# Hybrid attention layer on one core: two VectorE operations moved in the linear-attention steps, and the first projection begun on two token tiles

## The chip, the cores and the metric

The kernel runs on one core of a Trainium2 chip. The metric is device time in microseconds, from the start to the end of one execution; the median of several executions is given. TensorE multiplies matrices out of SBUF into PSUM, VectorE (DVE), ScalarE (ACT) and GpSimd (POOL) work elementwise, and SyncE (SP) issues the transfers. Each engine takes its instructions in order, and engines wait for one another through semaphores.

## The reference

One encoder layer on 1024 tokens of width 1024, all in float32. What matters here is the first part:

```python
h = rmsnorm(x, norm_mix_w[l])
proj = h @ w_in[l]
gq, gk, gv, ggate, ga, dq, dk, dv, dgate = split_cols(proj)
g = jax.nn.log_sigmoid((ga @ w_alpha2[l] + b_alpha2[l]).astype(f32)) / GLA_TAU
o_gla = gla_chunked(gq, gk, gv, g)          # chunks of 64 tokens, 4 heads
o_gla = head_rmsnorm(o_gla, gla_norm_w[l]) * jax.nn.silu(ggate)
# inside gla_chunked, per chunk
scores = jnp.where(causal, q_dec @ k_inv.T, 0.0)
o = scores @ v + q_dec @ state
state = decay * state + (k * jnp.exp(G_last - G)).T @ v
```

Behind it come differential attention over 4 heads, an output projection with residual, cross-attention into 256 memory tokens with its projections, and a last RMSNorm.

## The kernel before

Tokens are worked in 8 tiles of 128 (TT), the model width in 8 parts of 128 (KT). Each float32 operand of a large product is split in a high part and a low part: ScalarE writes the high part, VectorE subtracts it from the source for the low part (`lo_part`), and TensorE makes three matmuls (`mm3`): high by high, high by low, low by high. A weight matrix comes in tiles of 128x512, loaded by SP into a ring of four (`w_raw`) and split into a ring of 13 (`w_hi`, `w_lo`); a slot of `w_raw` is loaded again when the low part of the tile four before is done.

The order of the whole program is one list of stages, `PLAN`, written by `stages()` with the weight tiles (`("w", n)`) put in by `with_weights()`. Every engine walks through this one list and issues its own share of each stage, so the place of a stage in the list sets its place in each engine's queue. The stages that matter here:

- `("sq", t)`, `("scale", t)`: squares of input tile t (ScalarE), variance (VectorE), its root (GpSimd), scaling (VectorE). `("tr", t, half)`: four transposes on TensorE, high part on ScalarE, low part on VectorE, into `actT_hi` and `actT_lo`.
- `("busy", part, n)`: n transposes of the identity on TensorE, which nobody reads.
- `("pos",)`, `("vec",)`: positions converted on VectorE; norm weights, gate bias and positions turned on TensorE and copied to `vecs` and `pos_f` on VectorE. Every weight tile is scaled by a column of `vecs`.
- `("const",)`: the 16 gate columns of `w_in`, scaled and split into `ga_both`. `("ga", n)`: product of `ga_both` with 512 tokens. `("z", n)`: gate logits, `("gate", n)`, `("gsum", n)`, `("gexp", n)`: log-sigmoid, running sums and exponentials.
- `("G0", n, k)`: part k of the projection of q and k of the linear attention, for 512 tokens, into four PSUM banks.
- Linear attention in 16 steps (`GLA_STEPS`): two pairs of heads, eight tiles of 128 tokens each. Per step s: `("sc", s)`, scores on TensorE, their masked copy out of PSUM on VectorE (`sc_f`), high part on ScalarE, low part on VectorE; `("kv", s)`, chunk states; `("qk", s + 1)` and `("kdT", s + 1)`, operands of the next step; `("proj", s + 1)`, projection of the next values and gate path (24 matmuls of 512 columns) into `bank0`, of which ScalarE takes v's high part and the tanh and VectorE v's low part; `("gmul", s + 1)`, the gate, after which `bank0` is free for the next projection; `("o", s)`, the output product, its sum out of PSUM (`o_f`) and squares; `("ovar", s)`, variance (`var_o`), with the root on GpSimd; `("ofin", s)`, output scaled by root and gate (`mix_out`, two operations), which SP stores to memory.

TensorE issues `kv` of a step only when v's low part is there (`v_dve`), and a projection when the gate before is done (`pj_dve`).

Of the kernel before, what the change touches and what calls it, by code (L numbers as in the profile page):

```python
# [23 lines left out]
F32 = mybir.dt.float32  # L24
# [54 lines left out]
def stages():  # L79
# [4 lines left out]
    def normed(t):  # L84
        return [("sq", t), ("scale", t)]

    def busy(part, n):
        return [("busy", part, n)]

    plan = [("zeros",), *normed(0), ("sq", 1), ("scale", 1), *normed(2), *busy(0, 24), *tr(0), *busy(1, 2), ("sq", 3), *tr(1)]  # L90
    plan += [("pos",), ("scale", 3), *busy(2, 4), *tr(2), *busy(3, 6), ("vec",), ("const",), *tr(3), *busy(4, 20), ("w", 0), ("w", 1), *normed(4), ("w", 2), *normed(5), ("ga", 0)]
    plan += [("w", 3), *normed(6), ("w", 4), *normed(7), ("G0", 0, 0), ("z", 0), ("gate", 0), ("G0", 0, 1), *tr(4)]
# [278 lines left out]
def build(nc, a, out):  # L371

    with ExitStack() as ctx:
# [78 lines left out]
        ga_both = sb("ga_both", [P, KT, P], F32R, zone_a)  # L452
# [72 lines left out]
        sq_sum, var_ok, rs_ok, scaled = sem("in_squares"), sem("in_var"), sem("in_rsqrt"), sem("in_scaled")  # L525
        tr_pe, tr_act, tr_dve = sem("inT_pe"), sem("inT_hi"), sem("inT_lo")
# [112 lines left out]
        def _(sp):  # L639
# [13 lines left out]
            for t in range(4):  # L653
                load_input(t)
# [10 lines left out]
            for n in range(2):  # L665
                load_weight(n)
# [67 lines left out]
        def _(pool):  # L734
# [15 lines left out]
            for stage in PLAN:  # L750
                kind, *w = stage
                if kind == "sq":
# [20 lines left out]
        def _(act):  # L773
# [21 lines left out]
            for stage in PLAN:  # L795
                kind, *w = stage
                if kind == "sin":
                    act.wait_ge(dve_c, 3)
# [11 lines left out]
                elif kind == "w":  # L810
# [5 lines left out]
                    if n == 7 * KT + 2 * 2 * KT:  # L816
                        act.wait_ge(dve_c, 5)
# [173 lines left out]
        def _(dve):  # L991
# [14 lines left out]
            for stage in PLAN:  # L1006
                kind, *w = stage
                if kind == "zeros":
                    dve.memset(ga_both[:, :, 2 * RANK:P].bitcast(F32), 0.0)
# [14 lines left out]
                elif kind == "const":  # L1024
                    dve.wait_ge(d_ga, 16 * 3)
                    then_wait(dve.tensor_tensor(ga_raw[:, :, :], ga_raw[:, :, :],
                                                nw_mix[:, :].unsqueeze(2).to_broadcast([P, KT, RANK]), ALU.mult))
                    ga_hi, ga_lo = ga_both[:, :, 0:RANK], ga_both[:, :, RANK:2 * RANK]
                    then_wait(dve.tensor_copy(ga_hi, ga_raw[:, :, :]))
                    lo_part(ga_lo, ga_raw[:, :, :], ga_hi).then_inc(dve_c, 1)  # L1030
# [132 lines left out]
                elif kind == "sc":  # L1163
# [5 lines left out]
                    last.then_inc(sc_cp, 1)  # L1169
                    dve.wait_ge(sc_act, s + 1)  # L1170
# [39 lines left out]
                elif kind == "proj":  # L1210
# [3 lines left out]
                    if i == 0:  # L1214
                        dve.wait_ge(dve_c, 4)
# [131 lines left out]
        def _(pe):  # L1347
# [56 lines left out]
            for stage in PLAN:  # L1404
# [21 lines left out]
                elif kind == "ga":  # L1426
                    n = w[0]
                    pe.wait_ge(dve_c, 1)
# [3 lines left out]
                    for k in range(KT):  # L1432
                        pe.matmul(banks[3], ga_both[:, k, :], actT_hi[:, k, c], start=k == 0, stop=False)
                        last = pe.matmul(banks[3], ga_both[:, k, :], actT_lo[:, k, c], start=False, stop=k == KT - 1)
                    last.then_inc(ga_pe, 1)
                elif kind == "z":
# [4 lines left out]
                    last.then_inc(z_pe, 1)  # L1441
                elif kind == "G0":
                    n, k = w
                    t = slice(512 * n, 512 * n + 512)
# [5 lines left out]
                    for c in range(4):  # L1450
                        if k == 0:
                            wait(pe, g0_dve, 4 * n + c - 3)
                        last = mm3(banks[4 + c], w_hi[:, k, cols(c)], w_lo[:, k, cols(c)],
                                   actT_hi[:, k, t], actT_lo[:, k, t], k == 0, k == KT - 1)
# [255 lines left out]
```

## Time and profile before

| what | value |
|---|---|
| median of 3 runs | 870.24 us (870.15 to 870.57) |
| profiled execution, own time | 874.1 us |
| its span | 872.4 us |
| TensorE busy | 850.4 us (97%) |
| VectorE busy | 529.6 us (61%) |
| ScalarE busy | 397.2 us (46%) |
| GpSimd busy | 44.1 us (5%) |
| granted TensorE clock, mean | 0.996 of 2.4 GHz |

The median stems from runs without a profile, all durations and starts from the one profiled execution, whose time is 3.9 us above the median. A timeline gives for each instruction its start from the begin of the span, its duration, engine and source line, and in brackets how long the engine sat idle ahead of it and for whom. PEld is the loading of TensorE's stationary operand. Many instructions overlap the one before on the same engine, so the distance of two starts can be shorter than a duration.

### The profile page before, as it was taken

The page shows a single profiled execution, that of the slowest core. Times are in us where ns is not written, and L with a number is a line of the kernel's source. Part 1 is how long each engine was busy: PE and PEld are TensorE (multiplying, and loading weights), DVE is VectorE, ACT ScalarE, POOL GpSimd, SP SyncE. Part 2 cuts the span into 40 slices and gives each one's busy share as a digit, 9 for nine tenths or more (in the row PEclk, how much of TensorE's full clock was granted, in tenths as well). Part 3 has the DMA queues.
Part 4 walks back from the last instruction along what each step waited for, and adds up shares of the span by engine and source line. Part 5 has one row for each costly group of instructions (what it writes and reads, how often), then busy time and mean ns, then how long its engine had stood idle before and what let it go on. Part 6 is the DMA issues. An engine that isn't in the chain of part 4 may idle for free.

```text
span 872.4 us, 12997 instructions
## 1 busy us (share of the span) xinstructions
PE 850.4 (97%) x4676; PEld 705.0 (81%) x4676; DVE 529.6 (61%) x1274; ACT 397.2 (46%) x982; POOL 44.1 (5%) x84
## 2 busy tenths in 40 slices
PE   7999999999999999999999899999999999999997
PEld 6777877777788888888878887888888888888885
DVE  6667667767578668678768765223336654355543
ACT  7765444444346345445545655203425543234422
POOL 2000000000000000000000000000100000010001
PEclk9999999999999999999999999999999999999999
DMA  8321112112212112102112266521022202351112
GB/s 270 110 78 37 31 41 69 37 43 67 59 31 55 35 34 56 34 22 67 43 63 74 88 213 216 184 86 61 32 89 74 68 29 73 97 192 49 49 49 97
DMA packets 53592, 67.69 MB, mean 78 GB/s; under 512 B 5844, under 2 KB 32536, under 8 KB 53528
## 3 DMA queue, kind: packets, MB, share of 16 engines
q1 hardware_dynamic: 53528, 66.85, 24.2%
q8 instruction: 38, 0.62, 0.3%
q14 instruction: 26, 0.21, 0.1%
HBM read 58.44 MB, written 8.39 MB: 77 GB/s over the span
## 4 chain that ended last, share of the span: by engine, by line
PE 78%; DVE 11%; ACT 4%; issue 3%; DMA 3%; POOL 0%; SPq 0%; POOLq 0%; ACTq 0%
PE bank L1350 12%; PE bank L1352 12%; PE bank L1351 12%; PE banks2to L1350 8%; PE banks2to L1352 8%; PE banks2to L1351 8%; PE banks6to L1401 4%; PE banks2to L1573 4%; PE bank L1599 2%; DVE w_lo L1004 2%; DVE state L1183 1%; ACT junk L789 1%; ACT w_hi L793 1%; DMA tile_a<-mixed 1%; DVE mix_out L1207 1%
## 5 line engine op out<-in xcount | busy, mean ns | idle before, releaser
L1350 PE MATMUL bank<-w_hi,actT_hi 128*128 128x512 f32 x472 | 189.8, 402 | 1.2 <-DVE gate L1161 0.3
L1352 PE MATMUL bank<-w_hi,actT_lo 128*128 128x512 f32 x472 | 184.5, 391 | 0.0
L1351 PE MATMUL bank<-w_lo,actT_hi 128*128 128x512 f32 x472 | 184.3, 390 | 0.0
L1004 DVE SCALAR_TENSOR_TENSOR w_lo<-w_raw,vecs,w_hi 128x512 fp32r<-128x512 f32 x120 | 86.6, 747 | 43.5 <-ACT w_hi L793 43.5
L1350 PEld LDWEIGHTS bank<-w_hi,actT_hi 128*128 128x128 f32 x472 | 88.9, 188 | 22.2 <-DVE gate L1161 3.5
L1352 PEld LDWEIGHTS bank<-w_hi,actT_lo 128*128 128x128 f32 x472 | 88.6, 188 | 19.2
L1351 PEld LDWEIGHTS bank<-w_lo,actT_hi 128*128 128x128 f32 x472 | 88.9, 188 | 16.6
L793 ACT ACTIVATE w_hi<-w_raw,vecs 128x512 fp32r<-128x512 f32 x120 | 82.4, 717 | 11.8 <-DMA w_raw<-in_w_cq 6.1
L1350 PE MATMUL banks2to<-w_hi,actT_hi 128*128 128x512 f32 x168 | 66.5, 396 | 0.0
L1352 PE MATMUL banks2to<-w_hi,actT_lo 128*128 128x512 f32 x168 | 65.6, 390 | 0.0
L1351 PE MATMUL banks2to<-w_lo,actT_hi 128*128 128x512 f32 x168 | 65.5, 390 | 0.0
L933 ACT ACTIVATE prob<-banks2to,neg_maxs 128x128 f32<-128x128 f32 (+7 forms) x64 | 46.9, 740 | 14.2 <-DVE neg_maxs L1247 13.9
L748 POOL TENSOR_TENSOR rs_o<-var_o,neg_half 128x1 f32<-128x1 f32 (+1 forms) x48 | 28.6, 596 | 413.0 <-DVE var_o L1272 271.8
L789 ACT ACTIVATE junk<-x_res 128x1024 bf16<-128x1024 f32 (+1 forms) x17 | 17.1, 1007 | 65.1 <-DVE x_res L1296 65.0
L1246 DVE TENSOR_REDUCE neg_max<-banks2to 128x2 f32<-128x256 f32 (+7 forms) x32 | 43.3, 1352 | 3.9 <-PE banks2to L1573 3.3
L1296 DVE TENSOR_TENSOR x_res<-banks2to,x_res 128x512 f32<-128x512 f32 x17 | 11.7, 691 | 46.8 <-PE banks2to L1352 46.8
L1350 PE MATMUL banks2to<-actT_hi,w_hi 128*128 128x512 f32 x96 | 38.8, 404 | 0.0
L1352 PE MATMUL banks2to<-actT_hi,w_lo 128*128 128x512 f32 x96 | 37.5, 391 | 0.0
L1351 PE MATMUL banks2to<-actT_lo,w_hi 128*128 128x512 f32 x96 | 37.4, 390 | 0.0
L1352 PEld LDWEIGHTS banks2to<-w_hi,actT_lo 128*128 128x128 f32 x168 | 31.5, 188 | 6.7
L793 ACT ACTIVATE qk_tok<-bank 128x192 f32<-128x192 f32 x28 | 9.3, 331 | 60.7 <-PE bank L1352 60.6
L1296 DVE TENSOR_TENSOR x_res<-bank,x_res 128x512 f32<-128x512 f32 x15 | 10.4, 691 | 43.4 <-PE bank L1352 43.4
(288 smaller groups left out, 1818.9 us busy)
## 6 DMA issues: line engine op xcount, KB each, us to landing
w_raw<-in_w_in SPq DMA_DIRECT2D x56, 256.0 KB, 2.9
w_raw<-in_w_ckv SPq DMA_DIRECT2D x32, 256.0 KB, 3.4
w_raw<-in_w_cq SPq DMA_DIRECT2D x32, 256.0 KB, 2.8
w_raw<-in_w_co SPq DMA_DIRECT2D x32, 256.0 KB, 2.7
stage_in<-in_x SPq DMA_DIRECT2D x8, 512.0 KB, 4.9
tile_a<-mixed SPq DMA_DIRECT2D x16, 256.0 KB, 3.6
w_raw<-in_w_out SPq DMA_DIRECT2D x16, 256.0 KB, 3.1
x_res<-in_x SPq DMA_DIRECT2D x8, 512.0 KB, 4.9
```

The lines of the kernel that those rows point to most:

```text
L748: pool.tensor_tensor(dst, src, neg_half[:, 0:n], ALU.pow).then_inc(sem_out, 1)
L789: act.activation(junk[:, 0:n], src, ACT.Square, accum_out=total).then_inc(sem_done, 1)
L793: return act.activation(dst, src, ACT.Copy, scale=scale)
L933: last = act.activation(prob[:, m, 0:n], wide[:, 2 * m:2 * m + 2, :].rearrange("p j c -> p (j c)")[:, 0:n], ACT.Exp, scale=DQK ** -0.5, bi ...
L1004: return dve.scalar_tensor_tensor(dst, src, scale, hi.bitcast(F32), ALU.mult, ALU.subtract)
L1246: then_wait(dve.tensor_reduce(neg_max[:, i % 2, :], both, AX.X, ALU.max, negate=True))
L1296: dve.tensor_tensor(x_res[:, t, c], ps, x_res[:, t, c], ALU.add).then_inc(pr_dve, 1)
L1350: pe.matmul(dst, l_hi, r_hi, start=start, stop=False)
L1351: pe.matmul(dst, l_hi, r_lo, start=False, stop=False)
L1352: return pe.matmul(dst, l_lo, r_hi, start=False, stop=stop)
L1401: last = pe.transpose(ps[:, cols(j)], src, ident[:, :])
L1573: last = pe.matmul(wide[:, 2 * half + g // 512, 0:keys.stop - g], l[rows, 0, cols(t)], r[rows, 1, keys], start=m == 0, stop=m == 2)
```

## The change

Three edits. In the linear-attention steps the scores' masked copy is a stage of its own, `("scp", s)`, ahead of `("ovar", s - 1)`, and `("ofin", s - 1)` stands ahead of `("proj", s + 1)`. At the start the first two parts of the q and k projection are done on two token tiles (256 tokens) first, as `("G0h", k)`, ahead of the gate projection, and their `("G0", 0, k)` covers the other 256 tokens; the stages around are put in another order, the fourth input tile is loaded behind the small vectors and the first weight tile, and there are 42 instead of 56 filler transposes. The splitting of the gate weights goes from VectorE to GpSimd, and `ga_both` has 32 columns instead of 32 and 96 zeros.

```diff
-    plan = [("zeros",), *normed(0), ("sq", 1), ("scale", 1), *normed(2), *busy(0, 24), *tr(0), *busy(1, 2), ("sq", 3), *tr(1)]
-    plan += [("pos",), ("scale", 3), *busy(2, 4), *tr(2), *busy(3, 6), ("vec",), ("const",), *tr(3), *busy(4, 20), ("w", 0), ("w", 1), *normed(4), ("w", 2), *normed(5), ("ga", 0)]
-    plan += [("w", 3), *normed(6), ("w", 4), *normed(7), ("G0", 0, 0), ("z", 0), ("gate", 0), ("G0", 0, 1), *tr(4)]
+    plan = [("zeros",), *normed(0), *normed(1), ("sq", 2), *busy(0, 24), ("tr", 0, 0), ("pos",), ("scale", 2), ("tr", 0, 1)]
+    plan += [*busy(1, 2), ("tr", 1, 0), ("vec",), ("tr", 1, 1), *busy(2, 6), ("sq", 3), ("w", 0), ("tr", 2, 0), ("scale", 3)]
+    plan += [("tr", 2, 1), *busy(3, 10), ("G0h", 0), ("w", 1), *tr(3), ("G0h", 1), ("w", 2), ("const",)]
+    plan += [*normed(4), ("w", 3), *normed(5), ("ga", 0)]
+    plan += [("G0", 0, 0), ("z", 0), *normed(6), ("w", 4), *normed(7), ("gate", 0), ("G0", 0, 1), *tr(4)]
...
     for s in range(GLA_STEPS):
+        plan.append(("scp", s))
         if s:
             plan.append(("ovar", s - 1))
...
-            plan.extend([("proj", s + 1), *passed, ("gmul", s + 1), ("o", s)])
+            plan.extend([*passed, ("proj", s + 1), ("gmul", s + 1), ("o", s)])
...
-        ga_both = sb("ga_both", [P, KT, P], F32R, zone_a)
+        ga_both = sb("ga_both", [P, KT, 2 * RANK], F32R, zone_a)
...
+                if kind == "const":
+                    pool.wait_ge(d_ga, 16 * 3)
+                    pool.wait_ge(vec_dve, 1)
+                    pool.tensor_tensor(ga_raw[:, :, :], ga_raw[:, :, :],
+                                       nw_mix[:, :].unsqueeze(2).to_broadcast([P, KT, RANK]),
+                                       ALU.mult).then_inc(ga_pool, 1)
+                    pool.wait_ge(ga_pool, 1)
+                    pool.tensor_copy(ga_both[:, :, 0:RANK], ga_raw[:, :, :]).then_inc(ga_pool, 1)
+                    pool.wait_ge(ga_pool, 2)
+                    pool.tensor_tensor(ga_both[:, :, RANK:2 * RANK], ga_raw[:, :, :],
+                                       ga_both[:, :, 0:RANK].bitcast(F32), ALU.subtract).then_inc(ga_pool, 1)
...
+                elif kind == "G0h":
+                    k = w[0]
+                    if k == 0:
+                        pe.wait_ge(tr_dve, at("tr", 1, 1))
+                        pe.wait_ge(vec_dve, 1)
+                    pe.wait_ge(w_dve, k + 1)
+                    for c in range(4):
+                        mm3(banks[4 + c][:, 0:256], w_hi[:, k, cols(c)], w_lo[:, k, cols(c)],
+                            actT_hi[:, k, 0:256], actT_lo[:, k, 0:256], k == 0, False)
```

How instructions stand on the engines. TensorE at the start, before the change, from the third input tile (`stage_in`) to the gate projection (`ga_both`):

```order
L1423 MATMUL bank<-ident,stage_in 128x128 x8
L1409 MATMUL banks6to<-ident 128x128 x6
L1414 MATMUL banks2to<-ident,vec_rows 128x28
L1415 MATMUL banks2to<-ident,pos_rows 128x8
L1423 MATMUL banks2to<-ident,stage_in 128x128 x8
L1409 MATMUL banks6to<-ident 128x128 x20
L1433 MATMUL banks2to<-actT_hi,ga_both 128x512
L1434 MATMUL banks2to<-actT_lo,ga_both 128x512
```

And after it, from the first half of the second input tile to the first matmuls of a half projection (`w_hi`), 12 of them for each of the two:

```order
L1433 MATMUL banks2to<-ident,stage_in 128x128 x4
L1424 MATMUL banks2to<-ident,vec_rows 128x28
L1425 MATMUL banks2to<-ident,pos_rows 128x8
L1433 MATMUL banks2to<-ident,stage_in 128x128 x4
L1419 MATMUL banks6to<-ident 128x128 x6
L1433 MATMUL bank<-ident,stage_in 128x128 x8
L1419 MATMUL banks6to<-ident 128x128 x10
L1360 MATMUL banks2to<-actT_hi,w_hi 128x256
L1361 MATMUL banks2to<-actT_lo,w_hi 128x256
L1362 MATMUL banks2to<-actT_hi,w_lo 128x256
```

The vectors' transposes moved into the second input tile's, and the half projections stand where the gate projection stood, which now follows the second of them.

VectorE in a linear-attention step with one weight tile, before the change:

```order
L1004 SCALAR_TENSOR_TENSOR w_lo<-w_raw,vecs,w_hi 128x512
L1197 TENSOR_SCALAR var_o<-sq_o 128x2
L1167 COPY_PREDICATED sc_f<-gla_mask,banks2to 128x128 x2
L1003 TENSOR_TENSOR sc_lo<-sc_f,sc_hi 128x256
L1183 SCALAR_TENSOR_TENSOR state<-state,decay,banks2to 128x256 x2
L1003 TENSOR_TENSOR st<-state,st 128x256 x2
L1003 TENSOR_TENSOR q_lo<-q_dec,q_hi 128x2x64
L1003 TENSOR_TENSOR k_lo<-k_inv,k_hi 128x128
L1003 TENSOR_TENSOR ke_lo<-bank,ke_hi 128x128
L1003 TENSOR_TENSOR v<-bank,v 128x256
L1207 SCALAR_TENSOR_TENSOR mix_out<-o_f,rs_o,gate 128x128 x2
L1161 SCALAR_TENSOR_TENSOR gate<-tanh_g,bank 128x256
```

And after it:

```order
L1020 SCALAR_TENSOR_TENSOR w_lo<-w_raw,vecs,w_hi 128x512
L1175 COPY_PREDICATED sc_f<-gla_mask,banks2to 128x128 x2
L1207 TENSOR_SCALAR var_o<-sq_o 128x2
L1019 TENSOR_TENSOR sc_lo<-sc_f,sc_hi 128x256
L1193 SCALAR_TENSOR_TENSOR state<-state,decay,banks2to 128x256 x2
L1019 TENSOR_TENSOR st<-state,st 128x256 x2
L1019 TENSOR_TENSOR q_lo<-q_dec,q_hi 128x2x64
L1019 TENSOR_TENSOR k_lo<-k_inv,k_hi 128x128
L1019 TENSOR_TENSOR ke_lo<-bank,ke_hi 128x128
L1217 SCALAR_TENSOR_TENSOR mix_out<-o_f,rs_o,gate 128x128 x2
L1019 TENSOR_TENSOR v<-bank,v 128x256
L1169 SCALAR_TENSOR_TENSOR gate<-tanh_g,bank 128x256
```

Two pairs changed places: `sc_f` and `var_o`, and `mix_out` and v's low part.

## Rows read from the trace of the kernel before

**Rows 1.** Page, part 1: busy time (share of the span) and instructions of each engine.

```profile
PE 850.4 (97%) x4676; PEld 705.0 (81%) x4676; DVE 529.6 (61%) x1274; ACT 397.2 (46%) x982; POOL 44.1 (5%) x84
```

**Rows 2.** Timeline 0 to 30 us, TensorE: start, duration (us), engine, line, operation, out<-in.

```profile
17.76 0.47 PE L1433 MATMUL banks2to<-actT_hi,ga_both 128*128 128x512 f32 x1 [0.29 <-DVE actT_lo L1003]
...
26.21 0.50 PE L1350 MATMUL banks2to<-actT_hi,w_hi 128*128 128x512 f32 x1
...
29.07 1.03 PE L1423 MATMUL bank<-ident,stage_in 128*128 128x128 f32 x8
```

**Rows 3.** Timeline 0 to 30 us, the other engines; in brackets idle time before.

```profile
9.21 1.06 ACT L793 ACTIVATE actT_hi<-bank 128x512 fp32r<-128x512 f32 x2
...
10.16 1.05 ACT L789 ACTIVATE junk<-stage_in 128x1024 bf16<-128x1024 f32 x1
...
12.24 0.55 POOL L748 TENSOR_TENSOR rs_in<-var_in,neg_half 128x1 f32<-128x1 f32 x1 [2.12 <-DVE var_in L1074]
...
13.40 0.73 DVE L1079 TENSOR_SCALAR stage_in<-stage_in,rs_in 128x1024 f32<-128x1024 f32 x1
...
15.55 0.28 DVE L1026 TENSOR_TENSOR ga_raw<-ga_raw,vecs 128x128 f32<-128x128 f32 x1
15.86 1.33 ACT L793 ACTIVATE w_hi<-w_raw,vecs 128x512 fp32r<-128x512 f32 x2
...
16.33 1.28 DVE L1003 TENSOR_TENSOR actT_lo<-banks2to,actT_hi 128x512 fp32r<-128x512 f32 x2
...
17.53 1.41 DVE L1004 SCALAR_TENSOR_TENSOR w_lo<-w_raw,vecs,w_hi 128x512 fp32r<-128x512 f32 x2
```

**Rows 4.** Timeline 121.5 to 138 us: a linear-attention step with one weight tile, from gate to gate.

```profile
125.41 0.42 DVE L1161 SCALAR_TENSOR_TENSOR gate<-tanh_g,bank 128x256 f32<-128x256 f32 x1
...
128.62 0.16 DVE L1197 TENSOR_SCALAR var_o<-sq_o 128x2 f32<-128x2 f32 x1
128.69 0.49 DVE L1167 COPY_PREDICATED sc_f<-gla_mask,banks2to 128x128 f32<-128x128 uint32 x2
...
132.18 0.38 ACT L866 ACTIVATE tanh_g<-bank 128x256 f32<-128x256 f32 x1
...
132.30 0.28 DVE L1003 TENSOR_TENSOR ke_lo<-bank,ke_hi 128x128 fp32r<-128x128 f32 x1
...
132.59 0.42 DVE L1003 TENSOR_TENSOR v<-bank,v 128x256 fp32r<-128x256 f32 x1
...
132.93 0.60 DVE L1207 SCALAR_TENSOR_TENSOR mix_out<-o_f,rs_o,gate 128x128 f32<-128x128 f32 x2
...
133.12 0.51 PE L1509 MATMUL banks2to<-v,ke_hi 64*128 64x256 f32 x4
...
133.57 0.42 DVE L1161 SCALAR_TENSOR_TENSOR gate<-tanh_g,bank 128x256 f32<-128x256 f32 x1
...
134.05 0.19 PEld L1350 LDWEIGHTS bank<-w_hi,actT_hi 128*128 128x128 f32 x1 [0.24 <-DVE gate L1161]
```

**Rows 5.** VectorE's gates, by their source line: durations (min/median/max ns), first and last start.

```profile
L1161 DVE SCALAR_TENSOR_TENSOR gate<-tanh_g,bank x16: 410/420/422, 85.3 to 206.8; 128x256 f32<-128x256 f32 x16
```

**Rows 6.** Timeline 108 to 118.5 us: a step without a weight tile.

```profile
109.81 0.50 PE L1350 MATMUL bank<-w_hi,actT_hi 128*128 128x512 f32 x1
...
116.27 0.42 DVE L1003 TENSOR_TENSOR v<-bank,v 128x256 fp32r<-128x256 f32 x1 [1.05 <-ACT tanh_g L866]
...
117.36 0.33 PE L1466 MATMUL bank<-ident,k_end 128*128 128x128 f32 x1
...
117.73 0.50 PE L1350 MATMUL bank<-w_hi,actT_hi 128*128 128x512 f32 x1
```

**Rows 7.** Timeline 141 to 152 us: ScalarE in the step with three weight tiles.

```profile
146.25 0.42 ACT L793 ACTIVATE sc_hi<-sc_f 128x256 fp32r<-128x256 f32 x1 [0.64 <-DVE sc_f L1167]
```

**Rows 8.** Timeline 650.9 to 654 us, TensorE: first 256-column score matmul, and what follows 24 of them.

```profile
651.00 0.28 PE L1350 MATMUL banks2to<-ck_hi,cq_hi 128*128 128x256 f32 x1
...
653.87 0.40 PE L1350 MATMUL bank<-actT_hi,w_hi 128*128 128x512 f32 x1
```

More of the change, by code:

```diff
@@ L525, in build @@
         sq_sum, var_ok, rs_ok, scaled = sem("in_squares"), sem("in_var"), sem("in_rsqrt"), sem("in_scaled")
+        ga_pool = sem("gate_weights_split")
         tr_pe, tr_act, tr_dve = sem("inT_pe"), sem("inT_hi"), sem("inT_lo")
@@ L651, in load_weight @@
                     sp.dma_start(dst, src).then_inc(d_raw[n % NRAW], 16)
-            for t in range(4):
+            for t in range(3):
                 load_input(t)
@@ L664, in _ @@
                 sp.dma_start(dst, src).then_inc(d_vec, 16)
-            for n in range(2):
-                load_weight(n)
+            load_weight(0)
+            load_input(3)
+            load_weight(1)
             for dst, src in (
@@ L751, in _ @@
                 kind, *w = stage
-                if kind == "sq":
+                if kind == "const":
[9 more added lines that the diff above has]
+                                       ga_both[:, :, 0:RANK].bitcast(F32), ALU.subtract).then_inc(ga_pool, 1)
+                elif kind == "sq":
                     c = slice(w[0], w[0] + 1)
@@ L797, in _ @@
                 if kind == "sin":
-                    act.wait_ge(dve_c, 3)
+                    act.wait_ge(dve_c, 2)
                     act.activation(sin2[:, :, :, :], ang2[:, :, :, :], ACT.Sin).then_inc(act_c, 1)
@@ L816, in _ @@
                     if n == 7 * KT + 2 * 2 * KT:
-                        act.wait_ge(dve_c, 5)
+                        act.wait_ge(dve_c, 4)
                     _, scale = weight_tile(n)
@@ L1008, in _ @@
                 if kind == "zeros":
-                    dve.memset(ga_both[:, :, 2 * RANK:P].bitcast(F32), 0.0)
                     dve.memset(row_pick[:, :], 0.0)
@@ L1023, in _ @@
                     dve.tensor_copy(pos_f[:, :], banks[5][:, 28:36]).then_inc(vec_dve, 1)
[L1024 to L1030, printed above, removed]
                 elif kind == "ang":
@@ L1162, in _ @@
                                              bank0[:, 256:512], ALU.add, ALU.mult).then_inc(pj_dve, 1)
-                elif kind == "sc":
+                elif kind == "scp":
                     s = w[0]
@@ L1169, in _ @@
                     last.then_inc(sc_cp, 1)
+                elif kind == "sc":
+                    s = w[0]
                     dve.wait_ge(sc_act, s + 1)
@@ L1214, in _ @@
                     if i == 0:
-                        dve.wait_ge(dve_c, 4)
+                        dve.wait_ge(dve_c, 3)
                     dve.wait_ge(pj_act, s + 1)
@@ L1427, in _ @@
                     n = w[0]
-                    pe.wait_ge(dve_c, 1)
+                    pe.wait_ge(ga_pool, 3)
+                    pe.wait_ge(d_ga, 16 * 3)
                     pe.wait_ge(tr_dve, at("tr", 4 * n + 3, 1))
@@ L1432, in _ @@
                     for k in range(KT):
-                        pe.matmul(banks[3], ga_both[:, k, :], actT_hi[:, k, c], start=k == 0, stop=False)
-                        last = pe.matmul(banks[3], ga_both[:, k, :], actT_lo[:, k, c], start=False, stop=k == KT - 1)
+                        pe.matmul(banks[3][0:2 * RANK, :], ga_both[:, k, :], actT_hi[:, k, c],
+                                  start=k == 0, stop=False)
+                        last = pe.matmul(banks[3][0:2 * RANK, :], ga_both[:, k, :], actT_lo[:, k, c],
+                                         start=False, stop=k == KT - 1)
                     last.then_inc(ga_pe, 1)
@@ L1441, in _ @@
                     last.then_inc(z_pe, 1)
+                elif kind == "G0h":
[7 more added lines that the diff above has]
+                            actT_hi[:, k, 0:256], actT_lo[:, k, 0:256], k == 0, False)
                 elif kind == "G0":
                     n, k = w
-                    t = slice(512 * n, 512 * n + 512)
+                    half = ("G0h", k) in NTH and n == 0
+                    t = slice(512 * n + 256 * half, 512 * n + 512)
                     if k == 0:
@@ L1452, in _ @@
                             wait(pe, g0_dve, 4 * n + c - 3)
-                        last = mm3(banks[4 + c], w_hi[:, k, cols(c)], w_lo[:, k, cols(c)],
-                                   actT_hi[:, k, t], actT_lo[:, k, t], k == 0, k == KT - 1)
+                        last = mm3(banks[4 + c][:, 256 * half:512], w_hi[:, k, cols(c)], w_lo[:, k, cols(c)],
+                                   actT_hi[:, k, t], actT_lo[:, k, t], k == 0 and not half, k == KT - 1)
                         if k == KT - 1 and n + c < 4:
```

## The prediction

> **What bounds the kernel now.** I read the page first: TensorE is busy 850.4 us of a span of 872.4 us [rows 1], and with 97% there is no stage in which another engine sets the time for long. What can be won is what TensorE spends at the start without real work, and the small gaps between its stages. So I read next the timeline of the first 30 us [rows 2, 3], and then the timeline of the linear-attention steps [rows 4 to 7], because the change touches these two stretches alone.
>
> The start: the first matmul that computes something is that of the gate projection at 17.76 us [rows 2]. Until then TensorE turns input tiles and otherwise turns the identity to stay busy, and these filler turns count as busy. What it waits for is a chain on ScalarE and VectorE: squares, scaling, high parts, low parts. The last link before 17.76 is the low part of the fourth token tile, 16.33 to 17.6 us, and directly ahead of it VectorE prepares the gate weights from 15.55 us [rows 3].
>
> The linear-attention steps: VectorE's gates start between 85.3 and 206.8 us, sixteen of them [rows 5]. A step that also prepares one weight tile takes 133.57 - 125.41 = 8.16 us [rows 4]. By the program there are ten of these behind the second gate, three steps without a tile (117.73 - 109.81 = 7.92 us from projection to projection [rows 6]), and one with three tiles. Inside a step the chain is gate, sum of the output's halves, squares, w_hi, w_lo, variance, masked scores' copy, sc_hi, and so on until v's low part, mix_out, gate. In a step of 8.16 us TensorE starts the next projection at 134.05, 0.06 us behind the end of the gate (133.57 + 0.42) [rows 4], and the row says that it sat idle for 0.24 us until that gate. So this loop is set by VectorE and ScalarE, not by TensorE.
>
> **The change, part one: the start.** First the times up to the first half projection. ScalarE has the squares of tile 2 behind it and copies tile 0's high parts at 9.21 to 10.2 us, as now [rows 3]. The first half of tile 1 follows to 10.8. TensorE's transposes of the vectors now stand between the two halves of tile 1, and wait for VectorE's conversion of the positions, which stands behind one low part: 9.8 + 0.6 + 0.2 = 10.6 us. That makes the second half of tile 1 ready on TensorE at about 11.4 instead of 10, and copied at 12.0. Then the squares of tile 3 (1.05 plus 0.2 for the read [rows 3]) end at 13.1; w_hi of weight tile 0 (1.33 for two, so 0.7 [rows 3]) ends at 13.8, w_lo at 14.55. The half projection of weight tile 0 starts at 14.6. It has 12 matmuls of 256 columns. The nearest rows are those of the cross-attention scores, 24 such matmuls in 653.87 - 651.00 = 2.87 us [rows 8], 0.12 each: 1.44 us, until 16.1.
>
> Then to the gate projection. VectorE goes on without a pause from 13.85: w_lo 0.67, low part 0.60, scaling 0.67, low part 0.60, w_lo 0.67, two low parts 1.24 (issue intervals by [rows 3]), which ends at 18.3. TensorE turns tile 3 to 17.1 and has the second half projection from 17.15 to 18.65. So the gate projection starts at 18.7, 0.94 us later than now, but with two half projections done. From there to the transposes of token tile 4 it takes 29.07 - 17.76 = 11.31 us now [rows 2]. Each of the two projections within it falls from 29.07 - 26.21 = 2.86 us to 1.44 + 0.14, so 2.56 us less: 8.75 us. Tile 4 is reached at 27.45 instead of 29.07: a gain of **1.6 us**. Behind that TensorE is without a gap, and the weight tiles and low parts that it needs are one to several us early, so the gain stays. The removed memset and the 32 instead of 128 columns of the gate weights cost and give nothing: a matmul is priced by its moving columns, and those stay 512.
>
> GpSimd takes over the gate weights: three operations on 128x128. They may start at about 13.9, behind the fourth root of a variance, and are wanted at 18.7, so they have 4.8 us. No row shows such an operation there. Bounds: from below, VectorE's same product at 0.28 us [rows 3]; from above, GpSimd's power of one element per partition takes 0.55 [rows 3], and if each element cost that much it would be 70 us. It is nearest to an ordinary elementwise product, so I take 0.5 us each: 1.5 us, hidden. The next variance behind it in GpSimd's queue comes at 19.4 us and doesn't wait.
>
> The Trainium skill, GPSIMD Engine Reference, section 3.1 on elementwise cycle accounting, gives about 2.6 cycles per element for an operation with two inputs. As an estimate from that page, 128 elements at 1.2 GHz are 0.28 us and a dispatch on top; by it the three would be hidden too. No run here shows it yet.
>
> The SP queue: tile 3 is loaded behind the vectors and weight tile 0, some 1.3 us later than now. Now its squares start at 10.16, without a wait [rows 3]; they will start at 12.0. Covered; without that cover it costs what it is late.
>
> **Part two: a step of the linear attention.** Two instructions move on VectorE; TensorE's order stays. (a) The scores' copy goes ahead of the variance. Now the variance starts at 128.62, the copy at 128.69 [rows 4]: 0.07 us leave the loop. The variance falls into the time in which VectorE waits for sc_hi. (b) mix_out goes ahead of v's low part. This part starts at 132.59, though ke_lo started at 132.30 and such operations follow each other at 0.20: it waited 0.09 us for tanh, which ends at 132.56 [rows 4]. mix_out waits for nothing, so it starts at 132.50, and tanh is covered by its 0.60. Another 0.09 us leave the loop: 8.16 becomes 8.00. But v's low part ends later: 0.64 behind, less 0.09. TensorE's kv product waits for it (it starts at 133.12, 0.11 behind that end [rows 4]), and without the idle 0.24 the projection would follow the kv product's start by 134.05 - 133.12 - 0.24 = 0.69, so the low part's end by 0.8 [rows 4]. That puts the projection some 0.40 us later against the gate, once and for all, not once a step, as long as the loop turns on VectorE. Is there room? In a step without a weight tile TensorE's last work, a transpose, starts at 117.36 and takes 0.14 to load, and the projection before started at 109.81 [rows 6]: without the last wait 7.7 us. With a wait ahead of the kv product that costs about 0.1, that is 7.8 against 8.0: 0.2 us of slack.
>
> So ten steps give 10 x 0.16 = 1.6 us. In the three steps without a tile VectorE idles before v's low part at 116.27; mix_out falls into that idle time, the gate ends near 117.03 instead of 117.67, and TensorE goes straight on behind its transpose (117.36 + 0.14 = 117.50 instead of 117.73) [rows 6]: 3 x 0.22 = 0.66 us. In the step with three weight tiles ScalarE sat idle 0.64 us for sc_f at 146.25, behind the variance's wait for the squares [rows 7]; with the copy first that goes: 0.6 us. Less the 0.40 once: 1.6 + 0.66 + 0.6 - 0.40 = **2.5 us**.
>
> Sum: 4.1 us. The profiled execution took 874.1 us, its span 872.4; it would become about 870.0 and 868.3. The median of the runs shown is 870.24, 3.9 below the profiled one; with the same difference it becomes **866.1 us**.
>
> **The rivals.** (1) The steps don't get shorter, because TensorE, now 0.40 later, is itself the limit: its 7.8 is close to 8.0, and a start behind a wait costs about 0.1 more. Then only the start gives: 868.6. (2) The start gives nothing, since w_lo of tile 0 or the second half projection come some 1.5 us later than worked out (the positions' wait in the middle of TensorE's queue is the likeliest place): 867.7. (3) GpSimd's reads hold up VectorE. The operations that follow 13.85 on VectorE end at 18.3, 0.35 before the gate projection, so a hold of three times 0.5 us costs 1.1 us: 867.2. No row shows GpSimd and VectorE in such work together, for or against. The Trainium skill, SBUF — State Buffer, on the shared port pair, says that a VectorE operation with two SBUF inputs and a GpSimd operation that reads SBUF exclude each other for the whole instruction; w_lo is one such. By it this rival would be the case. (4) mix_out isn't ready when its turn comes, so that v's low part waits for it behind tanh. Then projection, tanh, mix_out, low part, kv and projection close a loop: from the projection's start to the low part's end 116.27 + 0.42 - 109.81 = 6.88 [rows 6], with mix_out's 0.64 and the 0.80 to the projection 8.3 us in every step, 0.16 more in ten steps and 0.4 more in three, 2.8 us, and with the start 870.24 - 1.6 + 2.8 = 871.4. Against it: its variance starts at 128.62, four us before mix_out at 132.93 [rows 4], and a root takes 0.55 [rows 3]. (5) The slower side: GpSimd is slow. Each us that the three operations take beyond 4.8 delays the gate projection by one. From 4.8 + 4.1 = 8.9 us on, 3 us for each, the kernel is slower than before; at 4 us each it is 873.4. The power's 0.55 for one element speaks for it, the 0.28 of VectorE against it.
>
> **How the numbers follow.** Both parts as worked out: 0.50, own range 865.2 to 867.0. GpSimd's hold: 0.12 (867.2). Only the start: 0.12 (868.6). Only the steps: 0.12 (867.7). More than forecast, where TensorE's restarts behind waits become cheaper too: 0.07 (864.5). Loop through mix_out: 0.03. GpSimd slow: 0.04. The range 865.0 to 868.9 leaves out some 0.15. A difference of 0.2% (1.7 us) is about what can be told from no change; 868.5 and below is faster. Faster 0.84 (the forecast, the hold, the steps alone, the larger gain, and somewhat under half of the start alone, which lies at the bound), within 0.2% 0.11, slower 0.05.
>
> **What would show it.** In the changed profile: the first half projection near 14.6 us and the gate projection near 18.7; the transposes of token tile 4 near 27.5; gates 8.00 us apart in steps with one tile and 7.7 in the others; TensorE waiting before the kv product instead of before the projection; GpSimd's three operations together under 3 us. Wrong would make it: a GpSimd operation above 1.5 us, a half projection behind 16 us, granted clock under full speed while the half projections run (there is less filler ahead of them), or gates still 8.16 apart.

## The result

The changed kernel takes 864.12 us (median of four runs, 863.75 to 864.52) where the kernel before took 870.19 us beside it (four runs, 869.77 to 870.57): a ratio of 0.9928, with a 95% interval of 0.9914 to 0.9942, or 6.1 us less. It is faster, as forecast, but by 2.0 us more than the forecast of 4.1, and below the range.

The page of the changed kernel, profiled in an execution of 864.19 us with a span of 862.5 us, has this first part, to be held against [rows 1]:

```profile
PE 843.2 (98%) x4686; PEld 701.3 (81%) x4686; DVE 526.3 (61%) x1270; ACT 397.9 (46%) x982; POOL 46.1 (5%) x87
```

TensorE is busy for 98% of the span instead of 97%. Its busy time fell by 7.2 us and the span by 9.9 us, but a part of both comes from a dip that only the first profile of the kernel before has (told of below). Its timeline at the start, against [rows 2]:

```profile
14.11 0.36 PE L1360 MATMUL banks2to<-actT_hi,w_hi 128*128 128x256 f32 x1 [0.59 <-DVE w_lo L1020]
...
18.32 0.39 PE L1444 MATMUL banks2to<-actT_hi,ga_both 128*32 128x512 f32 x1
...
27.00 1.04 PE L1433 MATMUL bank<-ident,stage_in 128*128 128x128 f32 x8
```

The half projection stands at 14.11 (forecast 14.6), the gate projection at 18.32 (18.7), the transposes of tile 4 at 27.00 (27.45). From the second to the third it takes 8.68 us; 8.75 were worked out. The other engines there, against [rows 3]:

```profile
7.42 1.06 ACT L805 ACTIVATE junk<-stage_in 128x1024 bf16<-128x1024 f32 x1 [0.25 <-DMA stage_in<-in_x]
...
8.48 1.06 ACT L809 ACTIVATE actT_hi<-bank 128x512 fp32r<-128x512 f32 x2
...
13.21 0.75 DVE L1020 SCALAR_TENSOR_TENSOR w_lo<-w_raw,vecs,w_hi 128x512 fp32r<-128x512 f32 x1 [0.46 <-ACT w_hi L809]
13.35 0.87 POOL L760 TENSOR_TENSOR ga_raw<-ga_raw,vecs 128x128 f32<-128x128 f32 x1
...
14.28 0.29 POOL L764 CAST ga_both<-ga_raw 128x128 fp32r<-128x128 f32 x1
...
14.48 0.74 DVE L1087 TENSOR_SCALAR stage_in<-stage_in,rs_in 128x1024 f32<-128x1024 f32 x1
...
14.65 0.88 POOL L766 TENSOR_TENSOR ga_both<-ga_raw,ga_both 128x128 fp32r<-128x128 f32 x1
...
16.88 1.29 DVE L1019 TENSOR_TENSOR actT_lo<-banks2to,actT_hi 128x512 fp32r<-128x512 f32 x2 [0.40 <-ACT actT_hi L809]
```

A step with one weight tile, VectorE, ScalarE's tanh and TensorE, against [rows 4]:

```profile
121.00 0.28 DVE L1019 TENSOR_TENSOR ke_lo<-bank,ke_hi 128x128 fp32r<-128x128 f32 x1
121.05 0.38 ACT L882 ACTIVATE tanh_g<-bank 128x256 f32<-128x256 f32 x1
...
121.20 0.60 DVE L1217 SCALAR_TENSOR_TENSOR mix_out<-o_f,rs_o,gate 128x128 f32<-128x128 f32 x2
...
121.73 0.42 DVE L1019 TENSOR_TENSOR v<-bank,v 128x256 fp32r<-128x256 f32 x1
...
122.06 0.41 DVE L1169 SCALAR_TENSOR_TENSOR gate<-tanh_g,bank 128x256 f32<-128x256 f32 x1
...
122.25 0.50 PE L1532 MATMUL banks2to<-v,ke_hi 64*128 64x256 f32 x4 [0.17 <-issue]
...
122.80 0.33 PE L1489 MATMUL bank<-ident,k_end 128*128 128x128 f32 x1
122.88 0.48 PE L1360 MATMUL bank<-w_hi,actT_hi 128*128 128x512 f32 x1
...
125.26 0.50 DVE L1175 COPY_PREDICATED sc_f<-gla_mask,banks2to 128x128 f32<-128x128 uint32 x2
...
125.65 0.16 DVE L1207 TENSOR_SCALAR var_o<-sq_o 128x2 f32<-128x2 f32 x1
```

And the gates by their source line, against [rows 5]:

```profile
L1169 DVE SCALAR_TENSOR_TENSOR gate<-tanh_g,bank x16: 407/410/411, 83.2 to 199.9; 128x256 f32<-128x256 f32 x16
```

From the first to the last gate it takes 199.9 - 83.2 = 116.7 us instead of 121.5. A step with one tile takes 7.86 us (8.16 before, 8.00 forecast), one without 7.61 (7.92; 7.7), the one with three tiles 7.58 (8.36; 7.76). TensorE now waits ahead of the kv product (122.25, `issue`, 0.17 us) and no longer for the gate. The edits thus did what was foreseen, and the steps gave more.

The first profile of the kernel before was an unlucky execution in two ways: its input tile 2 landed late (e8), and its clock fell for a while (last section). A second profile of the same kernel (e0, below) has a span of 868.4 us, not 872.4, and the distance of spans is then 5.9 us, close to the 6.1 of the medians.

### The profile page after: what moved, and what is told of

Read it like the earlier page. It is cut to its first block, busy times and chain, and to the rows that moved or that the text cites. A ratio compares the mean times of both kernels' runs of the same rounds, so it can differ in the third digit from the quotient of the medians.

```text
span 862.5 us, 13019 instructions
## 1 busy us (share of the span) xinstructions
PE 843.2 (98%) x4686; PEld 701.3 (81%) x4686; DVE 526.3 (61%) x1270; ACT 397.9 (46%) x982; POOL 46.1 (5%) x87
## 4 chain that ended last, share of the span: by engine, by line
PE 90%; DVE 4%; DMA 2%; issue 2%; ACT 2%; POOL 0%; SPq 0%; POOLq 0%; ACTq 0%; DVEq 0%
PE bank L1360 15%; PE bank L1362 15%; PE bank L1361 15%; PE banks2to L1360 9%; PE banks2to L1362 8%; PE banks2to L1361 8%; PE banks6to L1411 4%; PE banks2to L1596 4%; PE bank L1622 2%; DVE w_lo L1020 1%; PE banks2to L1532 1%; DMA tile_a<-mixed 1%; PE banks6to L1362 1%; PE banks6to L1360 1%; PE banks6to L1361 1%
## 5 line engine op out<-in xcount | busy, mean ns | idle before, releaser
L1360 PE MATMUL banks2to<-actT_hi,w_hi 128*128 128x512 f32 (+1 forms) x100 | 39.7, 397 | 0.6 <-DVE w_lo L1020 0.6
L1362 PE MATMUL banks2to<-actT_hi,w_lo 128*128 128x512 f32 (+1 forms) x100 | 38.2, 382 | 0.0
L1361 PE MATMUL banks2to<-actT_lo,w_hi 128*128 128x512 f32 (+1 forms) x100 | 38.1, 381 | 0.0
```

The source lines that it names most:

```text
L1360: pe.matmul(dst, l_hi, r_hi, start=start, stop=False)
L1361: pe.matmul(dst, l_hi, r_lo, start=False, stop=False)
L1362: return pe.matmul(dst, l_lo, r_hi, start=False, stop=stop)
```

## The experiments

Medians are those of each kernel, with its ratio to the kernel before run beside it on the same chip (870.75 us for e0 to e3, 870.5 for e4 to e7, 870.25 for e8 to e10). Steps are distances of two gates. The changed kernel itself was timed in a group of its own, beside 870.19 us; since the kernel before moves between 870.19 and 870.75 us from group to group, a difference from the changed kernel's 864.12 us is uncertain by about half a microsecond.

### e0: the kernel before once more; e1: the steps' edits alone; e2: the start alone

e1 has from the change only this, with the masked copy as a branch of its own:

```diff
     for s in range(GLA_STEPS):
+        plan.append(("scp", s))
...
-            plan.extend([("proj", s + 1), *passed, ("gmul", s + 1), ("o", s)])
+            plan.extend([*passed, ("proj", s + 1), ("gmul", s + 1), ("o", s)])
```

e2 has the rest of it: order of the start, half projections, gate weights on GpSimd.

> The kernel before once more, profiled. In its first profile the part from 492 us on took 3.1 us longer than in the changed kernel, with the granted clock at 0.84 to 0.89 between 528 and 540 us. Theory: a rare dip of that one execution; then the span is 868.5 to 869.5 us and the clock over 0.99 there. Rival: the kernel before always loses it there; then the span is about 872 again.

> Only the two moves in the linear-attention steps, the start as before. Theory: the steps give 4.5 us whatever the start does, since the start hands on a shift: steps with one weight tile 7.86 us, without 7.61, time 870.2 - 4.5 = 865.7. Rival: the two parts help each other (the steps run from VectorE's loop only because TensorE comes early): time above 867.

> Only the new start, the steps as before. Theory: first gate at 83.2 us and steps at 8.16 and 7.92 us; 2.0 us, so 868.1. Rival: the 2 us are given back at the steps or the reloads: 869.5 or more.

Measured: e0 870.17 us. e1 866.41 us, 0.9948 [0.9936, 0.9961], 4.3 us less, steps of 7.87 and 7.60. e2 868.3 us, 0.9973 [0.9963, 0.9983], 2.4 us less with an interval of 1.5 to 3.2, steps of 8.16 and 7.92 as before. The two sum to 6.8 us, which their intervals let stand beside the 6.1 of the whole. So the 1.6 us forecast for the start lie inside its interval, and the 2.5 us forecast for the steps lie outside theirs (3.4 to 5.6): the excess is in the steps.

### e3: the scores' copy first, alone; e4: mix_out first, alone

e3 has the first line of the diff above, e4 the last two.

> Only the scores' copy ahead of the variance. Theory: 0.07 us in each of ten steps with one weight tile, up to 0.6 in the one with three tiles, nothing in the three without: 1.3 us, 868.9; steps of 8.09 us. Rival: the copy's place is worth the larger part of the 0.30 us a step (0.2 or more): 867.5 or less.

> Only mix_out ahead of v's low part. Theory: 0.09 us for the wait for tanh and 0.13 us because the gate, which waits for mix_out's end, no longer stands right behind it: 0.22 us in each of ten steps, 0.31 in the three without a weight tile, less 0.26 once: 2.9 us, 867.3; steps of 7.94 us. Rival: only the wait for tanh counts: steps of 8.07, 868.9.

Measured: e3 869.35 us, 0.998 [0.9971, 0.9989], steps of 8.09 with one tile and 7.92 with three. e4 866.79 us, 0.9959 [0.9947, 0.9972], steps of 7.94, 7.63 and 8.13. In a step with one tile the copy gives the 0.07 us that was forecast for it, and mix_out gives 0.22 where 0.09 was forecast; together they are 0.29 of the 0.30 us. In the step with three tiles the copy alone gives 8.36 - 7.92 = 0.44 us, less than the 0.6 forecast, mix_out alone 0.23, and both in one kernel 0.78. By its median e4 gained 3.7 us (2.4 to 4.6) where 2.9 were expected; the steps are as expected, and the rest lies inside the interval. VectorE in e4:

```profile
122.73 0.28 DVE L1003 TENSOR_TENSOR ke_lo<-bank,ke_hi 128x128 fp32r<-128x128 f32 x1
122.93 0.61 DVE L1207 SCALAR_TENSOR_TENSOR mix_out<-o_f,rs_o,gate 128x128 f32<-128x128 f32 x2
123.45 0.42 DVE L1003 TENSOR_TENSOR v<-bank,v 128x256 fp32r<-128x256 f32 x1
123.78 0.41 DVE L1161 SCALAR_TENSOR_TENSOR gate<-tanh_g,bank 128x256 f32<-128x256 f32 x1
```

From ke_lo at 122.73 to the gate it is 1.05 us, 0.20 + 0.52 + 0.33. Before the change the same four were 0.29 + 0.34 + 0.64 = 1.27 apart [rows 4]. From ke_lo to its follower it is 0.20 instead of 0.29, the forecast 0.09 of the wait for tanh. The other 0.13 is that mix_out is followed at 0.52, not 0.64. The program says what stood between: the gate's `wait(dve, of_dve, s - 1)`, since there are two slots for gates in turn, and this gate goes into the one that the mix_out directly ahead of it reads. There it waits for the end of mix_out; with v's low part between, that end has come.

### e5: a third slot for the gate

```diff
-                    wait(dve, of_dve, s - 1)
+                    wait(dve, of_dve, s - 2)
...
-                    dve.scalar_tensor_tensor(gate[:, 256 * (s % 2):256 * (s % 2) + 256], tanh_g[:, :], 1.0,
+                    dve.scalar_tensor_tensor(gate_slot(s), tanh_g[:, :], 1.0,
```

The kernel before, with the gate in three slots in turn (the third in a buffer that is idle then), so that the gate only has to wait for the mix_out of a step earlier, long done. The order is untouched.

> The kernel before with the gate in three places instead of two in turn, so that the gate need not wait for the end of the mix_out right ahead of it; the order stays. Theory: this wait costs 0.12 us a step: gate follows mix_out by 0.52 instead of 0.64, steps of 8.04 us, 10 x 0.12 and 3 x 0.12 in those without a tile: 1.6 us, 868.6. Rival: the wait costs nothing (the 0.64 is two operations' own time): 870.2 and steps of 8.16.

Measured: 869.12 us, 0.9985 [0.9976, 0.9994], so 1.4 us less (0.5 to 2.1) where 1.6 were expected. Two steps with one tile take 16.09 us, so 8.04 each: 0.12 less than 8.16, without anything moved. VectorE:

```profile
124.14 0.60 DVE L1213 SCALAR_TENSOR_TENSOR mix_out<-o_f,rs_o,gate 128x128 f32<-128x128 f32 x2
124.66 0.41 DVE L1167 SCALAR_TENSOR_TENSOR gate<-tanh_g,bank 128x256 f32<-128x256 f32 x1
```

The gate follows mix_out at 0.52. This is the term that the prediction lacked, by itself.

### e6: the wait put back into the changed kernel

```diff
+                    wait(dve, of_dve, s - 1)
```

ahead of v's low part, directly behind mix_out; nothing needs it there.

> The changed kernel with one wait more on VectorE: v's low part waits for the end of the mix_out ahead of it, as the gate did in the kernel before. Theory: steps with one weight tile go from 7.86 to 7.98 us, those without stay at 7.61: 1.2 to 1.4 us slower than the changed kernel, 865.4. Rival: no difference, 864.1.

Measured: 866.54 us, 0.9951 [0.9938, 0.9963], 2.4 us above the changed kernel where 1.2 to 1.4 were expected, and steps of 8.06:

```profile
121.81 0.61 DVE L1218 SCALAR_TENSOR_TENSOR mix_out<-o_f,rs_o,gate 128x128 f32<-128x128 f32 x2
122.53 0.42 DVE L1019 TENSOR_TENSOR v<-bank,v 128x256 fp32r<-128x256 f32 x1
122.87 0.41 DVE L1170 SCALAR_TENSOR_TENSOR gate<-tanh_g,bank 128x256 f32<-128x256 f32 x1
```

mix_out to v's low part is 0.72 instead of 0.53. (One step took 8.43; there v's low part sat idle 0.47 us for mix_out, the loop of rival 4, once. Ten steps at 0.20 and 0.37 more in that one are the 2.4 us.) The mechanism holds, and its size was missed: here it costs 0.19 to 0.20 a step, more than the 0.12 of before. Why the same wait is dearer ahead of v's low part than ahead of the gate was not tried.

### e7: the copy also ahead of w_lo

In the changed kernel the weight tiles of a step are put in behind `("scp", s)` instead of ahead of it:

```diff
+            n += plan[n + 1][0] == "scp"
```

> The changed kernel with the scores' copy also ahead of the step's weight tile on VectorE (w_lo), so that sc_hi needs not wait for it. Theory: VectorE's loop falls by about 1 us and TensorE becomes the bound of every step: all steps 7.6 us, ten times 0.25 us, 864.1 - 2.5 = 861.6. Rival: something else in the loop (squares, w_hi on ScalarE) keeps the steps at 7.8 or more: 863.5 or above.

Measured: 861.16 us, 0.989 [0.9875, 0.9905], 3.0 us below the changed kernel and the fastest of all. Every step takes 7.58 to 7.63:

```profile
120.93 0.42 DVE L1020 TENSOR_TENSOR v<-bank,v 128x256 fp32r<-128x256 f32 x1 [0.57 <-ACT tanh_g L883]
121.28 0.41 DVE L1170 SCALAR_TENSOR_TENSOR gate<-tanh_g,bank 128x256 f32<-128x256 f32 x1
...
128.88 0.41 DVE L1170 SCALAR_TENSOR_TENSOR gate<-tanh_g,bank 128x256 f32<-128x256 f32 x1
```

v's low part now waits 0.57 us for tanh, so for TensorE's projection, and TensorE's own rows show no idle time in this step: the loop is TensorE's, and 7.6 us is its floor. In the changed kernel there is no such idle time before 121.73: its 7.86 was still VectorE's and ScalarE's loop.

### e8: the fourth input tile loaded early; e9: gate weights on VectorE; e10: no half projections

All three are the changed kernel with one part undone. e8:

```diff
-            for t in range(3):
+            for t in range(4):
```

e9 has `("const",)` ahead of `*tr(3)` and its three operations on VectorE. e10:

```diff
-    plan += [("tr", 2, 1), *busy(3, 10), ("G0h", 0), ("w", 1), *tr(3), ("G0h", 1), ("w", 2), ("const",)]
+    plan += [("tr", 2, 1), *busy(3, 24), ("w", 1), *tr(3), *busy(4, 12), ("w", 2), ("const",)]
```

> The changed kernel, with the fourth input tile loaded ahead of the small vectors and the first weight tile again, as before the change. The profile of the changed kernel shows tile 2 ready for its squares at 7.42 us instead of 8.15, and everything behind it on ScalarE 0.7 us earlier, up to the first half projection at 14.1 instead of the forecast 14.6. Theory A: that earlier landing is where the start's unforeseen 0.4 us comes from. Then here the squares of tile 2 start at 8.1 again, the first half projection at 14.6 to 14.8, the gate projection at 18.7 to 19.0, and the time is 0.4 to 0.7 us above the changed kernel, so 864.5 to 864.8. Theory B: the landing doesn't matter, since the squares of tile 3, now free to come earlier, or the vectors' transposes set the half projection: then it stays at 14.1 and the time at 864.1. Theory C: the weight tile or the vectors, now behind 0.5 MB more, come so late that the vectors' transposes wait for them: over 865.5.

> The changed kernel, with the splitting of the gate weights on VectorE again (three operations, behind the low part of weight tile 1 and ahead of those of token tile 3). In the profile of before the three take about 0.28 us each with a wait for the end of each, some 0.8 to 0.9 us in all. Theory A: VectorE is what the gate projection waits for at the start, so it comes that much later, 19.2 instead of 18.3, and the time is 0.8 to 0.9 us above the changed kernel: 864.9 to 865.0. Theory B: the chain to the gate projection runs through TensorE (half projection, turns of tile 3), and VectorE has room: same time, 864.1. Theory C: GpSimd's operations held VectorE up in the changed kernel; then the move back gives part of it again, and the loss is under 0.5 us.

> The changed kernel without the two half projections: their 24 matmuls are filler again, and the two parts of the q and k projection cover 512 tokens each, behind the gate projection, as before the change. The new order of the input stages, the loading order and GpSimd's part stay. Theory A: of the start's gain of 2.0 us, the half projections are what is won (2.56 us of matmuls done ahead), and the new order costs 0.5 us on its own: then the gate projection is at 18.0 to 18.3, token tile 4 is turned at 29.3 to 29.6, and the time is 2.3 to 2.6 above the changed kernel: 866.4 to 866.7. Theory B: the new order gains by itself, since the gate projection then comes earlier without the second half projection ahead of it (17.0 to 17.5): then the loss is 1.3 to 1.8 us, 865.4 to 865.9.

Measured: e8 863.99 us (0.9923 [0.991, 0.9937]), e9 863.88 us (0.9923 [0.991, 0.9937]), both no different from the changed kernel; e10 866.49 us (0.9951 [0.9937, 0.9965]), 2.4 us above it.

e8, ScalarE's squares of tile 2 and the first half projection:

```profile
7.34 1.06 ACT L804 ACTIVATE junk<-stage_in 128x1024 bf16<-128x1024 f32 x1
...
14.21 0.35 PE L1359 MATMUL banks2to<-actT_hi,w_hi 128*128 128x256 f32 x1 [0.60 <-DVE w_lo L1019]
```

My theory fell: with the old order of loading the squares of tile 2 start at 7.34, not at 8.1, and the median stays where it was. In the six profiles of kernels with the old start these squares begin at 8.15, 7.17, 7.86, 8.10, 7.49 and 7.34 (before, e0, e1, e3, e4, e5), in the six with the new start and the new loading order between 7.03 and 7.42. Where they begin late (7.49 and above), ScalarE waits for the landing; at 7.34 and 7.17 they follow its own work, so the tile was there earlier still. The landing varies from one execution to the next, and the 8.15 that I worked from was the latest of them. Whether the new order also makes it earlier on average (7.2 against 7.7 us) is open: e8 is a single profile, and its median shows no loss.

e9, VectorE's last low part ahead of the gate projection, which follows:

```profile
16.95 1.28 DVE L1008 TENSOR_TENSOR actT_lo<-banks2to,actT_hi 128x512 fp32r<-128x512 f32 x2
...
18.39 0.40 PE L1440 MATMUL banks2to<-actT_hi,ga_both 128*32 128x512 f32 x1 [0.45 <-DVE actT_lo L1008]
```

The three operations take 16.95 - 16.09 = 0.86 us on VectorE, but 0.40 of them fall into the idle time that the changed kernel has at 16.88. The gate projection comes 4.58 us behind the first half projection (13.81) instead of 18.32 - 14.11 = 4.21, and the time doesn't show it (863.88 against 864.12 us). Moving the gate weights to GpSimd brought nothing that can be told.

e10, gate projection and tile 4:

```profile
18.03 0.39 PE L1444 MATMUL banks2to<-actT_hi,ga_both 128*32 128x512 f32 x1 [0.36 <-DVE actT_lo L1019]
...
29.34 1.04 PE L1433 MATMUL bank<-ident,stage_in 128*128 128x128 f32 x8
```

Without the half projections the gate projection comes only 0.29 us sooner than in the changed kernel, and tile 4 is 11.31 us behind it, instead of 8.68. So they cost 0.29 us, save 2.63, and are the whole gain of the start. Tile 4 at 29.34 is even 0.5 us later than the mean of the six profiles with the old start (28.8 us), which would be the cost of the new order; but that is one profile, and the medians don't show it: e10 has the steps of e1 and takes 866.49 us, e1 866.41.

## Why the change gave more than the prediction said

The failed step of the prediction is a term of the sum for part two: it took 0.64 us for the length of mix_out where mix_out takes 0.52 and a wait takes 0.12, and so gave each step that VectorE sets 0.16 us where the runs show 0.30. That term alone, 1.2 to 1.3 us over ten steps, is more than the 0.9 us by which the time lies below the range. The places, one by one:

**The start: 1.6 forecast, 2.0 between the two profiles compared, about 1.8 over all.** The first gate lies at a mean of 85.0 us in the six profiles with the old start and of 83.2 in six with the new (all but e10, which has no half projections). The step of the working that was off is "copies tile 0's high parts at 9.21 to 10.2 us, as now": ScalarE does that at 8.48, because in this execution the squares ahead of it could start 0.7 us sooner. That is the scatter of the landing told of at e8: as far as the runs show, the chance of one execution and not a gain of the change. From there on the sum held: from half projection to gate projection 4.1 forecast and 4.2 measured, from there to tile 4 8.75 and 8.68. The matmuls of 256 columns follow each other at 0.12, as read from [rows 8].

**The steps: 2.5 forecast, 4.6 between the profiles of e0 and the changed kernel, 4.3 timed alone (e1).** Here the step that failed is the sentence "But v's low part ends later: 0.64 behind, less 0.09". The 0.64 was taken for the length of mix_out's two operations and carried to their new place. It was 0.52 for mix_out and 0.12 for the gate's wait for its end (e5). That wait stands in the program; I had listed what VectorE waits for on other engines and not what it waits for on itself, where the rows show no idle time in brackets. It is 0.12 to 0.13 us in each step that VectorE sets. With the 0.07 and 0.09 that were forecast, and that e3 and e4 show, such a step saves 0.30 us, not 0.16, and ten of them 1.4 us more. In the step with three tiles 0.78 us were measured for 0.6 forecast. There the 0.6 was itself too large for the copy alone (0.44 in e3), and mix_out's 0.23 (e4), which holds this wait, made up for it: the forecast came near by luck.

**TensorE's floor: 7.7 forecast, 7.6 measured.** The step that was off is "a transpose, starts at 117.36 and takes 0.14 to load". The next load overlaps it: in the rows above the projection follows that transpose (122.80) at 0.08. Three steps without a tile gave 0.31, 0.32 and 0.34 us, not 0.22, which is 0.3 in all (0.2 against e0). By the same 0.06 the projection is 122.88 - 122.06 = 0.82 us behind the gate and not 0.48 + 0.40 [rows 4].

**The 0.40 us given back once: 0.1 measured.** From the first gate to the last, e0 takes 121.4 us and the changed kernel 116.7, which is 4.7 less; from the first gate to TensorE's first transposes of the next stage they take 129.65 and 125.04, which is 4.6 less. So 0.1 us is given back behind the steps. What takes up the rest of the later projection was not traced.

Against e0, which had its tile 2 early too, the sum closes: 1.6 for the start (84.8 to 83.2), 4.6 for the steps, 6.2 together, where the medians say 6.1 and the spans 5.9. The start's 1.6 is as forecast. Of the 2.1 us that the forecast of the steps lacked, about 1.4 stem from the ten steps with one tile (the wait for mix_out in the main), 0.2 from the three without, 0.2 from the one with three tiles and 0.3 from the smaller give-back.

**The other steps.** The profile's 3.9 us above the median did not touch the sum, as the same difference was taken for both, but 3.1 of them were the dip told of below: the stages of the changed kernel are 6.8 us ahead of that profile in front of it and 9.9 behind it. Rival 1 (only the start) falls with e1, rival 2 (only the steps) with e2. Rival 3, GpSimd holding VectorE, falls: w_lo at 13.21 runs beside GpSimd's product at 13.35 and takes 0.75 us, as in e9, where GpSimd is idle then, and what follows it starts 0.67 behind it here and 0.66 there. The Trainium skill, SBUF — State Buffer, "Who interferes with whom", would have the two exclude each other; no hold of VectorE is seen in this pair, in which VectorE was the first to start. The reverse order, a VectorE operation with two SBUF inputs issued while GpSimd reads, does not occur in this trace (the next w_lo starts at 15.74, behind GpSimd's end at 15.53), so the rival fell in part by that order. Whether GpSimd was held instead stays open (last section). Rival 4, the loop through mix_out, didn't come: v's low part follows mix_out without idle time. Rival 5, slow GpSimd: the operations take 0.87, 0.29 and 0.88 us instead of 0.5 each, 2.2 us from start to end, and are done 2.8 us before they are wanted. The case "more than forecast", with its 0.07, was the one that came, but by another cause than the cheaper restarts of TensorE that it named, for the most part: its 864.5 is near the measured 864.1 by luck.

## What to carry to other kernels

The distance of two starts on one engine is a length only where the second doesn't wait for the first; read the program for waits of an engine on its own results before pricing a swap, since the trace shows no idle time for waits as short as these. In these kernels such a wait cost something directly behind the operation that it is for (0.12 us a step, e5, and more where it is put back, e6), and an independent instruction between the two took it away (e4). And the start of this program varies by half a microsecond or more with the landing of transfers: with forecasts of 4 us a second profile of the kernel before is worth more than a third decimal of the first.

## What the runs showed of the hardware

A wait for the end of the operation directly ahead on VectorE cost 0.12 us (gate behind mix_out, e5) and 0.2 us (v's low part behind mix_out, e6). The Trainium skill, VectorE: DVE Perf Modes, "The DRAIN you can't avoid", measured eight copies in the same time with a semaphore after each and with one after the last alone, and says that the semaphore costs nothing extra there. By that the three-slot gate would have left a step at 8.16; the trace has 8.04, so for operations of this form the measurement decides.

GpSimd took 0.87 and 0.88 us for the elementwise operations with two inputs on 128x128, where VectorE took 0.29 (e9), and 0.29 for the cast. The Trainium skill, GPSIMD Engine Reference, section 3.1, gives about 2.6 cycles per element; the estimate of 0.28 us from it leaves 0.6 us. Whether these belong to the operation or are a hold is not shown. Both operations start while VectorE works on SBUF (w_lo from 13.21 to 13.96, the scaling of an input tile from 14.48 to 15.22) and end 0.26 and 0.31 us behind that work's end, as a hold would have it; they stand in nearly the same place to it in every profile with GpSimd's part, so no run tells the two apart, and 0.87 us is not a price to carry elsewhere.

The dip of the first profile of before: TensorE waited 1.86 us for a tile that it turns, and then ran at a lower clock. Its rows in that profile, and the stretch from 532 to 540 us (length, busy time of each engine, granted clock, DMA share, GB/s) there:

```profile
530.49 0.66 PE L1401 MATMUL banks6to<-ident,tile_a 128*128 128x128 f32 x4 [1.86 <-DMA tile_a<-mixed]
...
532.12 0.63 PE L1350 MATMUL banks2to<-w_hi,memT_hi 128*128 128x512 f32 x1
532.55 0.63 PE L1351 MATMUL banks2to<-w_lo,memT_hi 128*128 128x512 f32 x1
```

```profile
532.00:540.00 8.00, 8.00 (x33) 6.44 (x33) 4.42 (x7) 4.04 (x8) 0.00 (x0) 0.84 0.78 255
```

The matmuls follow each other at 0.43 us instead of 0.23, about half of full speed, until about 534.5. The granted clock is 0.50 of 2.4 GHz, so 1.2 GHz, from 532 to 534 us and 1.00 again from 535, and the mean of the stretch is 0.84. In e0 the same stretch of time has 1.00:

```profile
532.00:540.00 8.00, 8.00 (x38) 6.58 (x37) 4.87 (x8) 3.75 (x6) 0.00 (x0) 1.00 0.78 247
```

The wait alone doesn't decide it: in e4 TensorE waited 2.06 us for such a tile, and the granted clock of the 10 us around is 1.00:

```profile
506.84 0.66 PE L1401 MATMUL banks6to<-ident,tile_a 128*128 128x128 f32 x4 [2.06 <-DMA tile_a<-mixed]
```

```profile
502.00:512.00 10.00, 7.94 (x68) 7.74 (x67) 6.20 (x13) 5.39 (x10) 0.55 (x1) 1.00 0.65 215
```

What else it takes stays open.
